# The last merge pass of an encoder layer: gate products of tiles 2 to 7 computed ahead, in the differential attention and the DeltaNet, and their up products in one panel

## The reference, cut to what matters

```python
def gated_merge(h, branches, merge_w, merge_b, branch_up):
    out = None
    for i, y in enumerate(branches):
        term = jax.nn.sigmoid(h @ merge_w[i] + merge_b[i]) * (y @ branch_up[i])
        out = term if out is None else out + term
    return out
...
    merged = gated_merge(h, (y_gla, y_lru, y_diff, y_gdn), merge_w[l], merge_b[l], branch_up[l])
    x = x + merged @ mix_out[l]
```

## Time and profile before

| | |
|---|---|
| time, median of 3 runs | 2191.21 us (2190.84 to 2196.25) |
| profiled execution, its time | 2191.2 us |
| its span, first to last instruction | 2189.5 us |
| TensorE busy | 1970.5 us, 90% |
| VectorE busy | 1413.4 us, 65% |
| ScalarE busy | 1111.6 us, 51% |
| GpSimd busy | 270.8 us, 12% |
| mean granted clock of TensorE | 0.968 |

### The profile page before, as it was taken

How to read it: one execution, slowest core, us unless ns; L and a number is a source line. 1 busy time by engine, 2 the same in 40 slices (tenths; PEclk the granted TensorE clock), 3 DMA queues, 4 the chain that set the end, 5 groups by cost and what they waited for, 6 DMA issues and landing times. The chain is left out here.

```text
span 2189.5 us, 32211 instructions
## 1 busy us (share of the span) xinstructions
PE 1970.5 (90%) x12704; PEld 1188.9 (54%) x12704; DVE 1413.4 (65%) x1789; ACT 1111.6 (51%) x1602; POOL 270.8 (12%) x263
## 2 busy tenths in 40 slices
PE   5998999899998988899999999999599999999981
PEld 3455465555543546788447875578345445444440
DVE  5446533589974686544333374543689999999995
ACT  4462323466656431112423353343578888888863
POOL 1010000000100443341120000000100111111103
PEclk9999999999999999999999999999799999999995
DMA  4410101211001252221411241051599999999966
GB/s 166 161 49 29 36 23 58 73 44 49 25 25 44 88 181 75 85 59 35 164 44 49 77 141 39 6 182 44 205 363 422 423 422 422 422 422 422 422 272 240
DMA packets 138215, 356.21 MB, mean 163 GB/s; under 512 B 37968, under 2 KB 91376, under 8 KB 111472
## 3 DMA queue, kind: packets, MB, share of 16 engines
q1 hardware_dynamic: 94304, 273.27, 32.9%
q10 hardware_dynamic: 34944, 48.24, 6.4%
q0 software_dynamic: 8848, 33.03, 3.9%
HBM read 305.75 MB, written 44.56 MB: 160 GB/s over the span
## 5 line engine op out<-in xcount | busy, mean ns | idle before, releaser
L730 PE MATMUL psum<-arena 128*128 128x512 f16 (+2 forms) x6000 | 1017.5, 328 | 15.1 <-ACT arena L1301 5.4
L730 PEld LDWEIGHTS psum<-arena 128*128 128x128 f16 x6000 | 572.6, 99 | 402.2 <-issue 25.5
L1133 PE MATMUL psum<-arena 128*128 128x512 f16 x2304 | 513.9, 382 | 13.0 <-issue 9.9
L689 DVE SCALAR_TENSOR_TENSOR arena<-arena 128x2048 f16<-128x2048 f32 x192 | 437.2, 2285 | 66.6 <-ACT arena L684 66.4
L684 ACT ACTIVATE arena<-arena 128x2048 f16<-128x2048 f32 x192 | 365.3, 1908 | 65.6 <-DMA arena<-in_w_dram 35.2
L1133 PEld LDWEIGHTS psum<-arena 128*128 128x128 f16 x2304 | 224.9, 98 | 279.9 <-issue 21.3
L1853 DVE SCALAR_TENSOR_TENSOR arena<-arena 128x512 f16<-128x512 f32 (+1 forms) x212 | 141.4, 686 | 129.4 <-ACT arena L1283 129.1
L2703 POOL DMA_INDIRECT arena<-xhat,arena x32 | 65.8, 2056 | 849.2 <-PE psum L1122 446.5
L1283 ACT ACTIVATE arena<-arena 128x512 f16<-128x512 f32 (+1 forms) x212 | 127.0, 616 | 44.2 <-issue 11.5
L2600 POOL TENSOR_TENSOR arena<-arena 128x512 f32<-128x512 f32 x48 | 66.3, 1381 | 581.9 <-DVE arena L1872 581.9
L1301 ACT ACTIVATE arena<-psum,arena 128x512 f32<-128x512 f32 x64 | 43.8, 684 | 150.4 <-PE psum L730 150.1
(11 more groups left out here) (382 smaller groups left out, 2188.4 us busy)
## 6 DMA issues: line engine op xcount, KB each, us to landing
arena<-in_w_dram SPq DMA_DIRECT2D x192, 1024.0 KB, 11.9
arena<-in_merge_w_dram SPq DMA_DIRECT2D x64, 256.0 KB, 3.3
yrows<-arena ACTq DMA_DIRECT2D x32, 512.0 KB, 7.8
arena<-in_w_in_dram SPq DMA_DIRECT2D x48, 256.0 KB, 2.8
gdn_lq<-arena ACTq DMA_DIRECT2D x8, 1024.0 KB, 4.2
arena<-gdn_lq ACTq DMA_DIRECT2D x8, 1024.0 KB, 5.0
arena<-in_xattn_wkv_dram SPq DMA_DIRECT2D x32, 256.0 KB, 2.9
yrows<-arena POOLq DMA_DIRECT2D x1, 7680.0 KB, 24.4
```

Source lines behind the costliest of these rows:

```text
L689: nc.vector.scalar_tensor_tensor(half_of(XW[m][1], half), half_of(XLAND[m], half), WS, half_of(XW[m][0], half), ALU.mult, ALU.subtract).th ...
L730: mm = nc.tensor.matmul(bank[prt[0]:prt[1], c0:c1], lhs[a](k), rhs[b](k), start=(k == 0 and a + b == 0), stop=(k == nk - 1 and a == 1))
L1133: mm = nc.tensor.matmul(PS[:, bank, :], left[a][:, k, :], right[b][:, k, columns], start=k + a + b == 0, stop=(k == n - 1 and a == 1))
```

## The change

The gates of branch D for tiles 2 to 7 (12 groups, 48 parts) leave `merge(3)`. They become three panels of their own, `early1` (tiles 2 and 3), `early2` (4 and 5), `early3` (6 and 7), each with 16 parts and four chunks of weights. `early1` follows `merge(0)` and lies in the attention, `early2` and `early3` follow `merge(2)` and lie in the DeltaNet. ScalarE evacuates an early gate into `SG` as before, waits for its own evacuation and stores the 256 KB to memory outside the core, `early_gates`; the next gate but one waits for that store. At `x_again` ScalarE issues 12 loads of the early gates ahead of the eight loads of x. `merge(3)` keeps the panel `merge30` (tiles 0 and 1, gates and ups). Behind it comes one panel `late3`: three chunks of up weights and the 12 up products of tiles 2 to 7, one part each. VectorE takes the gates from where they were loaded, and waits once for all 12 loads. `merged_pair` j - 1 now follows the evacuation of the second half of up product j. All 1681 steps of the list remain 1681.

The places: one more part after the value product of every even block of the attention (16); in the DeltaNet one more before the first `gdn_a` part 1, one more behind `gdn_a` part 0 of chunks 1 to 7, one more behind `gdn_out` of chunks 1 to 7, three more between inverses, three and three more around the loads of the inverses (24 in all), and one more behind `gdn_c` part 1 of each chunk (8). Since the added parts push the others forward, every product of `merge(0)` and `merge(2)` stands at an earlier place of its branch than before.

```diff
+EARLY = (2, 3, 4, 5, 6, 7)
+LATE = (0,)
...
-        for q in range(4):
+        for q in range(4) if i != 3 else LATE:
...
+            if (i, q) == (3, 0):
+                add("late3", [(up[:, :, 128 * j:128 * j + 256], j - EARLY[0], 0) for j in EARLY[::2]],
+                    [("up", 3, j, half) for j in EARLY for half in range(2)])
+
+    def early(*qs):
+        for q in qs:
+            add(f"early{q}", [(kview(A["merge_w"][3])[:, :, q * 256:q * 256 + 256], 0, 0)],
+                [("gate", 3, 2 * q + jt, half) for jt in range(2) for half in range(2)])
...
-                    if kind == ("gate", 3, kind[-2], 0) and kind[-2] and part == 2:
+                    if kind == ("gate", 3, kind[-2], 0) and kind[-2] not in (0,) + EARLY and part == 2:
                         steps.append(("merged_pair", kind[-2] - 1))
+                    if kind[:2] == ("up", 3) and kind[2] in EARLY and kind[3] == 1:
+                        steps.append(("merged_pair", kind[2] - 1))
...
-        diff += [None] + [("diff_comb", u + 1)] * more + [("diff_pv", u)] + [None] * (u % 2)
-    dense(*merge(0), between=diff)
+        diff += [None] + [("diff_comb", u + 1)] * more + [("diff_pv", u)] + [None] * 1
+    dense(*merge(0), *[f"early{q}" for q in (1,)], between=diff)
...
-        gdn += [("gdn_a", i, 1)] + {6: inv(0, 1), 7: inv(0, 4)}.get(i, []) + [None] + [("gdn_a", i + 1, 0)] * (i + 1 < TT) + mid
-        gdn += [("gdn_a", i, 2), ("gdn_out", i)] + [("gdn_ship", 0)] * (i == 3) + [None]
+        gdn += [("gdn_a", i, 1)] + {6: inv(0, 1), 7: inv(0, 4)}.get(i, []) + [None] + [("gdn_a", i + 1, 0), None] * (i + 1 < TT) + mid
+        gdn += [("gdn_a", i, 2), ("gdn_out", i)] + [("gdn_ship", 0)] * (i == 3) + [None] * (1 + (i > 0))
...
-        gdn += inv(0, p) + [None] * 2 + [("gdn_load", p - 5)] * (p < 7)
-    gdn += [("gdn_back", 0)] + [None] * 3 + [("gdn_load_inv", 0), ("gdn_load_inv", 1), ("gdn_read", 1)] + [None] * 4
+        gdn += inv(0, p) + [None] * (2 + (p < 8)) + [("gdn_load", p - 5)] * (p < 7)
+    gdn += [("gdn_back", 0)] + [None] * 6 + [("gdn_load_inv", 0), ("gdn_load_inv", 1), ("gdn_read", 1)] + [None] * 7
...
-            gdn += [("gdn_c", i, part)] + [None] * (2 <= part < 6)
+            gdn += [("gdn_c", i, part)] + [None] * (1 <= part < 6)
...
-    dense("nq", "nk", "nv", *merge(2), between=gdn)
+    dense("nq", "nk", "nv", *merge(2), *[f"early{q}" for q in (2, 3)], between=gdn)
...
+        def early_gate(kind):
+            return f32(BR + 4096 * kind[3] + 512 * kind[2], 512)
...
+                        if n in early:
+                            act.wait_ge(*e.at(n))
+                            S.dma_start(A["early_gates"][early.index(n)], SG[slot]).then_inc(gate_out[slot], 16)
...
+                    for s in range(2):
+                        act.wait_ge(gate_out[s], 16 * len(early) // 2)
+                    for m, n in enumerate(early):
+                        S.dma_start(early_gate(kind_of[n]), A["early_gates"][m]).then_inc(gate_in, 16)
                     for tt in range(TT):
                         S.dma_start(X[:, tt, :], A["x"][tt * P:tt * P + P, :]).then_inc(x_again, 16)
...
+                        gate = SG[gate_no[gate_of(n)] % 2]
+                        if gate_of(n) in early:
+                            gate = early_gate(kind)
+                            dve.wait_ge(gate_in, 16 * len(early))
```

23 lines of the change are left out of this document (17 added, 6 removed).

## The result

The changed kernel takes 2203.69 us (median of 11 runs, 2198.28 to 2207.42) where the kernel before took 2190.84 beside it: ratio 1.0049, interval 1.0036 to 1.0062. It is slower by 12.9 us; the prediction said 26.5 us faster, and 2203.69 lies outside its range. The profiled execution is the median one, with a span of 2201.9 us. The page's first part says little: TensorE is busy 8 us longer than in the earlier trace rows.

What follows compares the result with a forecast made beforehand. The prediction took TensorE, busy 90% of the span, as the bound, with VectorE bounding some stretches. It summed -62.3 + 8 + 8.1 + 4.5 + 8.2 + 7 = -26.5 us, from 2191.2 to 2164.7 us, range 2145 to 2184.

Steps and rivals of the forecast that it cites:

- What bounded the kernel, and the unit: Whole kernel: TensorE busy 90% of the span; a part takes 1.297 us, so 48 parts take 62.3 us off the last merge.
- 16 parts in the attention, +8: Attention: 20.8 us of added parts mostly fill TensorE's waits; blocks go from 6.60 to 6.85 us, plus 8 us.
- the attention takes nothing: Rival, attention: any delay of the transposes lengthens the loop, all 20.8 us show; 2177.5 us, chance 0.20.
- 24 parts around the first pass, +8.1: DeltaNet's first pass, inverses and way back: of 31.1 us of parts, plus 8.1 us shows, bounds 0 and 18.
- 12.4 us idle and slow: First pass up to 785: TensorE's 8.0 us idle plus 4.4 of slow clock, counted as room for 13.0 us of parts.
- One such stall stays: First pass: one up product again lands where the next mask waits, so one stall, 7.1 us with its clock, remains.
- 2.1 + 0.8 - 2.5: From 785 to the second pass: 2.1 us VectorE work, 0.8 left of parts on the way back, 2.5 clock gain.
- 8 parts in the second pass, +4.5: DeltaNet's second pass: 10.4 us of parts behind gdn_c part 1 partly fill waits, plus 4.5 us, bounds 0 and 10.4.
- x_again, +8.2: Step x_again: 12 gate loads on ScalarE's queue cost 5.7 us, lower clock 2.5; plus 8.2 us, bounds 4 and 10.
- the panel, +7: Panel of 12 up products: VectorE and GpSimd hinder each other; plus 7 us over TensorE's 15.6, bounds 2 and 12.
- the two rivals above it: Whole kernel: no net effect, about 70% shows, within 6.6 us of 2191.2, chance 0.07; slower, 2206.4 us, chance 0.05.
- the parts stand ahead of what all wait for: Rival, all three stages: each part lengthens a loop over the engines by its whole 1.30 us; 2206.4 us, chance 0.05.

Runs made afterwards that it cites:

- e3_filler: Kernel before plus 6 unread filler matmuls at each of the 16 added attention places, its own parts unmoved: 20.8 us of TensorE work cost 5.0 us.
- The two shifts: Kernel before with every merge(0) product one or three parts earlier against the attention's blocks, no work added: attention 26.3 and 39.7 us longer.
- the filler: Kernel before plus 6 zero-operand matmuls at the 24 places added around the DeltaNet's first pass: 19.9 of the 25.3 us came with TensorE's time alone.
- k3_gates_first: Kernel moving only tiles 4 to 7's gates, with both early panels ahead of merge(2): first pass and inverses 132.2 us, second pass 198.1 us.
- e1_no_attention: Changed kernel without its attention part: tiles 4 to 7 early in the DeltaNet, tiles 2 and 3 in the last merge; 2194.5 us.
- k1_tiles_6_7: Only tiles 6 and 7's gates moved (16 parts), attention and first pass as in the kernel before, gate loads by SP's queue: 2216.5 us.
- e6_exp_first: Changed kernel with each attention block's exponential step ahead of the part that stood before it: attention 255.8 us.
- e12_shift_3: Kernel before with three more places for parts ahead of the attention's first step, no work added: attention 39.7 us longer.

## Why the prediction was wrong

**What bounded the kernel, and the unit**: right. The 48 parts were TensorE time: the 45.1 us that the merge gave and the 14.8 us found below for `x_again` and the panel make 59.9 of the 62.3; 2.4 us are not placed.

**16 parts in the attention, +8; it was +21.9.** This is the first failed step. The sum priced the added 16 parts and asked whether they fit into TensorE's gaps; they did (5.0 us in `e3_filler`, by the step "where a wait is as long as that at 488.50 the part fits"). What it did not price is that every other product moved. The section on the change says that every product of `merge(0)` stands at an earlier place than before; the sum gave it nothing. The two shifts priced it: 26 and 40 us for a pattern out of step. The upper bound of 20.8, "nothing is absorbed", was no bound. The rival "the attention takes nothing" has nearly the right size and, in the main, the wrong reason: the added part by itself cost 5.0 us.

**24 parts around the first pass, +8.1; it was +25.3.** The second failed step, and of another kind. "12.4 us idle and slow" were set against 13.0 us of work, less one stall of 7.1, as if a part could be laid into any other idle time of the stretch. The windows show hardly any absorption in the chunks (14.95 of 15.6 us with the filler, and 8.9 us idle in the changed kernel where 8.0 were), since the long waits there end at something that itself starts from TensorE's products. "One such stall stays": there were two, as there had been before, and it is the up products beside the chunks that hold them open (`k3_gates_first`: 2.0 us idle with one add). Behind the last mask the idea was right and the size was not: about 0.4 us (2.1 + 0.8 - 2.5) predicted, 5.0 with the filler and 9.1 with parts; the clock there rose as foreseen (0.95 to 0.97, and 1.00 with the filler).

**8 parts in the second pass, +4.5; it was +2.0**, and in `e1_no_attention` the pass was 2.0 us shorter than before even with them. Right in direction, within what one profile tells; `k3_gates_first` and `k1_tiles_6_7` warn that this holds for gates and not with up products.

**x_again, +8.2, and the panel, +7.** The last merge gave 45.1 of 62.3 us, so 17.2 returned against 15.2. The wait grew from 1.37 to 7.72 us, 6.35, and the clock cost 1.5. The panel's rows are

```profile
1142.61 2.76 PE L752 MATMUL psum<-arena 128*128 128x512 f16 x12 [1.79 <-DVE arena L1909]
1145.63 1.47 PE L752 MATMUL psum<-arena 128*128 128x512 f16 x6 [0.26 <-DVE arena L1909]
...
1149.53 1.47 PE L752 MATMUL psum<-arena 128*128 128x512 f16 x6 [0.75 <-DVE arena L1909]
1151.20 1.47 PE L752 MATMUL psum<-arena 128*128 128x512 f16 x6 [0.20 <-DVE arena L1909]
...
1164.44 1.86 PE L752 MATMUL psum<-arena 128*128 128x256 f16 x8 [4.31 <-issue]
```

with eight waits of 4.9 us together and 4.31 in place of 2.29 at `mix0`: 6.9 us. Both terms held. The preparation's +2.1 was not in the sum.

**The range.** The sum of the terms' upper bounds is 71.2 - 62.3 = +8.9 us, not +6, and the range ended at -7, since it left out the two rivals above it. The measured +12.9 lies above both: the upper bounds of the attention (20.8) and of the first pass (18) were too low.

**The rivals.** The slower one, "the parts stand ahead of what all wait for", gave 2206.4 us and decided from "more than 47 of the 62.3 us": 51.2 showed, and the time was 2203.7. Its price and its threshold came out right, partly by luck: its mechanism holds for the chunks of the first pass, while in the attention it was not this, and the second pass gave next to nothing. It had a chance of 0.05, on the ground of 28 waits near the parts: waits that were read as room.

## What to carry to other kernels

Idle time of an engine is room only if what ends the wait does not itself start behind the place where work is added; follow the wait round to see whether it comes back to the engine, before setting work against it. Where a fixed filler pattern runs beside a periodic loop, their relative position is itself a tuned quantity: price what moves, not only what is added, and try the pattern shifted by a unit or two, which costs nothing to write. Look below a stage's total before calling a run for one side: two stretches in it can move against each other. And a queue that also issues transfers should do so behind the next thing that others wait for, not ahead of it.

## What was not expected of the hardware

That a position alone, with the same work on every engine, is worth 40 us of 232 (`e12_shift_3`), and that a VectorE operation on one element per partition takes 1.25 us instead of 0.22 when GpSimd's add of 128x512 starts just before it (539.67 above), in ten blocks of `e6_exp_first` 1.10 us or more. And that 12 issues of SP, 6.18 us, cost TensorE 14 us more than the same 12 on ScalarE's queue (a wait of 21.76 against 7.72 us), because a load of weights that was issued 24 us later came in beside 7 MB of others and took 14 to 15 us to land.
